# Opening of a transformer block on one core: four modulation blocks ahead of the first product instead of two

## The chip, the cores and the metric

One Trainium2 chip, one of its cores. The time is that of one execution on the device in microseconds, median of three runs. Engines are named as in the profile: PE is TensorE, ACT is ScalarE, DVE is VectorE, POOL is GpSimd, SP is SyncE, which issues most loads.

## The reference

The kernel computes one block of a transformer for 512 tokens of width 1024, in float32: a layer norm, a gated feed-forward (width 2816), a token mixer (pooling and three kinds of attention), and a second feed-forward, each followed by a layer norm and each entered by a modulation that depends on a vector c:

```python
x = layer_norm(x, ln_in_g, ln_in_b)
c_act = jax.nn.silu(c)
ada = (c_act @ w_ada[l] + b_ada[l]).reshape(c.shape[0], 3, 3, D_MODEL)
mod = lambda i, j: ada[:, i, j][:, None, :]
h = x * (1.0 + mod(0, 1)) + mod(0, 0)
x = layer_norm(ALPHA * x + 0.5 * mod(0, 2) * swiglu(h, ffn1_w_in[l], ffn1_w_out[l]), ln1_g[l], ln1_b[l])
```

The change is in what comes ahead of the first feed-forward and in its first products: the norm of x, mod(0, 0) and mod(0, 1) (shift and scale of h), and h itself.

## The kernel before

Everything is held transposed: X is eight tiles (m = 0 to 7) of 128 features x 512 tokens. A float32 product is made of three: a weight panel (128 x 1024, raw) is split into w_hi (ScalarE, L917) and w_lo (GpSimd, L433), h into h_hi (ScalarE, L967) and h_lo (VectorE, L1420), and TensorE multiplies h_hi by w_hi, h_lo by w_hi and h_hi by w_lo (L509 to L511, "a product" below: three matmuls). Raw panels have two slots, so panel p is loaded when panel p - 2 is split (L334).

**The order of the opening.** SyncE loads X in four pieces, then by the list FIRST_LOADS the panels ("p", i) of 512 KB and the modulation blocks ("a", k) of 1 MB (ada_first); block k holds the columns of w_ada that give shift and scale of tile k of h. TensorE sums X and its squares (first_norm, L559 and L561), turns the sums into columns (first_norm_columns, L570), VectorE makes mean and reciprocal deviation of them (with a square root on ScalarE), and TensorE spreads the two over all partitions (first_norm_row, L578, to banks 2 and 3).

For each block k: TensorE multiplies the block by c (first_modulation_rows, L540: 8 matmuls, 16 instructions), ScalarE copies the partial rows to arow (first_row, L942), TensorE sums them into columns (first_modulation_cols, L549), and VectorE makes mod of the columns (first_columns, L1410 to L1414; its last step counts up first_mod). Then ScalarE makes hbuf and h_hi of tile k (L962, L967), VectorE h_lo (L1420, which counts up h_split).

**The first products.** In feed_forward(1) six output tiles (banks 0 to 5) are summed at once, k outermost: for each k six products (18 matmuls), each waiting for h_split of its k. The eight panels' worth of weights is arranged so that the 48 products use panels 0 to 5 one after the other, eight products each. Rows of block k + AHEAD stand ahead of the products of k, its columns ahead of the product m = 3. AHEAD is 2, and the blocks use banks 6 and 7 in turn. ScalarE follows FIRST_SPLITS: behind first_row(k + AHEAD) it splits the panels listed for k and then makes h of tile k + 1. On all engines instructions are executed in the order of the program; each wait in it holds up what stands behind it on the same engine.

Behind the 48 products the feed-forward goes on with two banks at a time, and the rest of the kernel follows (mixer, second feed-forward).

Of the kernel before, what the change touches and what calls it, by code (L numbers as in the profile page):

```python
# [35 lines left out]
P = 128  # L36
D = 1024
T = 512
KT = D // P
# [55 lines left out]
FIRST_LOADS = [("p", 0), ("a", 0), ("a", 1), ("p", 1), ("a", 2), ("a", 3), ("p", 2), ("a", 4), ("a", 5), ("p", 3),  # L95
               ("a", 6), ("a", 7), ("p", 4), ("p", 5), ("p", 6)]

FIRST_SPLITS = [[1], [2], [3], [4], [], [5], [6], []]
AHEAD = 2
# [24 lines left out]
def build(nc, xT, cols, ada_w, ada1, ffn_in, ffn_out, mix_w, pool_w, branch_w, mixout_w,  # L124
          w1, w2, pos, ident_in, dist_in, cbias_in, cmask_in, icnt_in, out):
    with ExitStack() as ctx:
# [85 lines left out]
        ident_landed = sem("ident_landed")  # L212
# [118 lines left out]
        def _(sp):  # L331
# [54 lines left out]
            sp.dma_start(posv[:, :, :], pos[:, :, :]).then_inc(const_landed, 16)  # L386
            sp.dma_start(w2s[:, :, :, :], w2[:, :, :, :]).then_inc(const_landed, 16)
            sp.dma_start(icnt[:, :, :], icnt_in[:, :, :]).then_inc(const_landed, 16)
# [116 lines left out]
        def _(pe):  # L505
# [24 lines left out]
            def first_modulation_rows(k):  # L530

                b = 6 + k % 2
# [3 lines left out]
                if k >= 2:  # L536
                    pe.wait_ge(first_mod, k - 1)
# [6 lines left out]
            def first_modulation_cols(k):  # L544

                b = 6 + k % 2
# [48 lines left out]
            def feed_forward(n):  # L595
# [11 lines left out]
                for i in range(FIRST * KT):  # L607
# [5 lines left out]
                    if i == 1 and n == 1:  # L613
                        first_modulation_cols(1)
                    if m == 3 and n == 1 and k + AHEAD < KT:
                        first_modulation_cols(k + AHEAD)
                    if n == 1 and i == 2:
                        pe.wait_ge(rows_copied, 2)
                    if i % 8 == 0:
                        pe.wait_ge(split_done, base + i // 8 + 1)  # L620
# [41 lines left out]
            first_norm()  # L662
            first_norm_columns()
            first_modulation_rows(0)
            pe.wait_ge(ident_landed, 16)
# [3 lines left out]
            first_modulation_rows(1)  # L669
# [37 lines left out]
            pe.wait_ge(const_landed, 16 * 3)  # L707
# [196 lines left out]
        def _(act):  # L904
# [34 lines left out]
            def first_row(k):  # L939

                act.wait_ge(first_rows, k + 1)
                act.activation(arow[:, k, :], psum[:, 6 + k % 2, 0:2 * P],  # L942
                               ACT.Copy).then_inc(first_rows_taken, 1)

            def norm(L):

                act.wait_ge(var_done, L + 1)
                act.activation(st[:, 4, :], st[:, 3, :], ACT.Sqrt).then_inc(std_done, 1)
                if L == 0:
                    first_row(0)  # L950
# [6 lines left out]
                if L < 3:  # L957
# [11 lines left out]
                    if L == 0:  # L969
# [7 lines left out]
                        first_row(1)  # L977
                        todo[0] = 1
# [68 lines left out]
            act.dma_start(ident[:, :], ident_in[:, :]).then_inc(ident_landed, 16)  # L1047
# [133 lines left out]
        def _(dve):  # L1181
# [224 lines left out]
            def first_columns(k):  # L1406

                dve.wait_ge(first_cols, k + 1)
                shift_, scale_ = psum[:, 6 + k % 2, 2 * P:2 * P + 1], psum[:, 6 + k % 2, 2 * P + 2:2 * P + 3]
# [33 lines left out]
            first_low(0)  # L1443
            first_tile(1)
            first_columns(1)
            for m in range(1, KT):
# [3 lines left out]
                if m + 1 < KT:  # L1450
                    first_columns(m + 1)
# [318 lines left out]
```

## Time and profile before

| | us |
|---|---|
| median of 3 runs | 1177.31 (1176.4 to 1177.74) |
| the profiled execution | 1177.74 |
| its span, first to last instruction | 1175.6 |
| PE busy | 1117.5 (95%) |
| DVE busy | 522.4 (44%) |
| ACT busy | 399.7 (34%) |
| POOL busy | 540.8 (46%) |

The span is what the trace covers. A "PE busy" share of 95% is time in which some matmul was under way; matmuls overlap, so the start-to-start distance says more than the length of one. Times in a timeline count from the start of the span. A row of a timeline gives start and length in us, engine, line of the kernel, operation, what it writes and reads, how many; in brackets the idle time of the engine ahead of it and what ended that. Rows of loads give the time to issue in ns, first and last start in us, and the time from issue to landing. PEclk is the granted clock of TensorE as a share of 2.4 GHz.

### The profile page before, as it was taken

The numbers are of one execution on the slowest core, as the hardware profiler recorded it, in microseconds if no ns is written. First come the engines' busy times: TensorE is split into PE (matmuls) and PEld (weight loads), VectorE is DVE, ScalarE is ACT, GpSimd is POOL, SyncE is SP. The second block draws the span as 40 slices with busy tenths as digits, with TensorE's granted clock in tenths as the row PEclk, the third lists the DMA queues.
The fourth block names the chain that finished last, engine by engine and source line by source line (L and its number), as shares of the span: only waits on it lengthen the run. The fifth ranks groups of instructions, "written<-read, shape, count | busy, mean of one in ns | idle before, by whom it ended". The sixth has DMA issues, their size and how long they took to land.

```text
span 1175.6 us, 14482 instructions
## 1 busy us (share of the span) xinstructions
PE 1117.5 (95%) x5184; PEld 885.3 (75%) x5184; DVE 522.4 (44%) x829; ACT 399.7 (34%) x608; POOL 540.8 (46%) x268
## 2 busy tenths in 40 slices
PE   7999999999999699999999999969999999999992
PEld 4788888888888477865478888848888888888881
DVE  5577776111311564268837776661622221111116
ACT  4453322323222352247722233344323232222212
POOL 2434555444444352357815553544544544444423
PEclk9999999999999799999999999979999999999996
DMA  9455554323233621110036554313333332333311
GB/s 372 158 189 196 188 187 154 105 85 96 86 99 101 225 85 47 57 55 18 19 117 215 189 183 138 125 36 126 125 125 125 107 114 100 88 96 99 99 32 72
DMA packets 46991, 142.06 MB, mean 121 GB/s; under 512 B 5472, under 2 KB 5984, under 8 KB 45664
## 3 DMA queue, kind: packets, MB, share of 16 engines
q1 hardware_dynamic: 45936, 136.25, 35.0%
q10 hardware_dynamic: 1008, 5.17, 1.1%
q8 instruction: 30, 0.49, 0.2%
q14 instruction: 17, 0.14, 0.0%
HBM read 139.31 MB, written 2.10 MB: 120 GB/s over the span
## 4 chain that ended last, share of the span: by engine, by line
PE 77%; issue 10%; POOL 5%; DVE 5%; ACT 2%; DMA 0%; POOLq 0%; ACTq 0%; DVEq 0%
PE psum L509 24%; PE psum L511 24%; PE psum L510 24%; POOL w_lo L433 3%; PE psum L694 1%; POOL Pr L468 1%; POOL h_lo L491 1%; PE psum L593 1%; ACT Pr L1113 1%; PE psum L813 1%; DVE X L1284 1%; PE psum L526 0%; DMA X<-in_xT 0%; PE psum L540 0%; PE psum L762 0%
## 5 line engine op out<-in xcount | busy, mean ns | idle before, releaser
L433 POOL TENSOR_TENSOR w_lo<-raw,w_hi 128x1024 fp32r<-128x1024 f32 x184 | 453.7, 2471 | 547.6 <-ACT w_hi L917 547.3
L509 PE MATMUL psum<-h_hi,w_hi 128*128 128x512 f32 x952 | 375.3, 394 | 9.0 <-POOL h_lo L491 8.8
L511 PE MATMUL psum<-h_hi,w_lo 128*128 128x512 f32 x952 | 372.3, 391 | 0.0
L510 PE MATMUL psum<-h_lo,w_hi 128*128 128x512 f32 x952 | 372.2, 391 | 0.0
L917 ACT ACTIVATE w_hi<-raw 128x1024 fp32r<-128x1024 f32 x184 | 192.6, 1051 | 162.2 <-PE psum L511 103.2
L509 PEld LDWEIGHTS psum<-h_hi,w_hi 128*128 128x128 f32 x952 | 179.8, 189 | 54.9 <-POOL h_lo L491 9.5
L511 PEld LDWEIGHTS psum<-h_hi,w_lo 128*128 128x128 f32 x952 | 179.8, 189 | 38.1
L510 PEld LDWEIGHTS psum<-h_lo,w_hi 128*128 128x128 f32 x952 | 179.9, 189 | 36.5
L1312 DVE SCALAR_TENSOR_TENSOR acc<-ada_raw,cact,acc 128x512 f32<-128x512 f32 x98 | 145.3, 1517 | 19.3 <-DMA ada_raw<-in_ada_w 19.2
L509 PE MATMUL psum<-act_hi,w_hi 128*128 128x512 f32 x352 | 137.3, 390 | 0.0
L511 PE MATMUL psum<-act_hi,w_lo 128*128 128x512 f32 x352 | 137.0, 389 | 0.0
L510 PE MATMUL psum<-act_lo,w_hi 128*128 128x512 f32 x352 | 136.9, 389 | 0.0
L1380 DVE SCALAR_TENSOR_TENSOR X<-psum,mod,X 128x512 f32<-128x512 f32 x24 | 18.0, 750 | 217.4 <-PE psum L511 217.4
L1015 ACT ACTIVATE act_hi<-scr 128x512 f32 (+1 forms) x42 | 26.5, 632 | 194.2 <-DVE scr L1342 194.2
L1333 DVE SCALAR_TENSOR_TENSOR scr<-scr,psum 128x512 f32<-128x512 f32 x44 | 30.2, 686 | 108.6 <-ACT scr L1022 108.6
L511 PEld LDWEIGHTS psum<-act_hi,w_lo 128*128 128x128 f32 x352 | 66.1, 188 | 13.8
L510 PEld LDWEIGHTS psum<-act_lo,w_hi 128*128 128x128 f32 x352 | 66.1, 188 | 13.6
L509 PEld LDWEIGHTS psum<-act_hi,w_hi 128*128 128x128 f32 x352 | 66.1, 188 | 13.5
L1342 DVE TENSOR_TENSOR scr<-scr,psum 128x512 f32<-128x512 f32 x44 | 30.2, 686 | 89.0 <-PE psum L511 88.7
L1022 ACT ACTIVATE scr<-psum 128x512 f32<-128x512 f32 x44 | 26.0, 592 | 85.1 <-PE psum L511 85.1
L468 POOL TENSOR_SCALAR Pr<-Pr,pscl 128x128 f32<-128x128 f32 (+2 forms) x48 | 44.9, 954 | 19.2 <-DVE pscl L1585 19.2
L1324 DVE TENSOR_TENSOR act_lo<-scr,act_hi 128x512 f32 (+1 forms) x44 | 35.6, 808 | 36.7 <-ACT act_hi L1015 35.3
(205 smaller groups left out, 960.1 us busy)
## 6 DMA issues: line engine op xcount, KB each, us to landing
raw<-in_ffn_in SPq DMA_DIRECT2D x88, 512.0 KB, 3.3
ada_raw<-in_ada_w SPq DMA_DIRECT2D x112, 256.0 KB, 3.6
raw<-in_mix_w SPq DMA_DIRECT2D x31, 512.0 KB, 3.3
raw<-in_ffn_out SPq DMA_DIRECT2D x32, 448.0 KB, 3.3
ada_first<-in_ada SPq DMA_DIRECT2D x8, 1024.0 KB, 11.6
raw<-in_ffn_out SPq DMA_DIRECT2D x16, 512.0 KB, 3.5
raw<-in_branch_w SPq DMA_DIRECT2D x8, 512.0 KB, 4.0
raw<-in_mixout_w SPq DMA_DIRECT2D x8, 512.0 KB, 3.3
```

What stands on the lines that cost most here:

```text
L433: gp.tensor_tensor(w_lo[:, slot, :], raw[:, slot % 2, :], w_hi[:, slot, :].bitcast(F32), ALU.subtract).then_inc(split_done, 1)
L468: gp.tensor_scalar(pr, pr, pscl[:, n:n + 1], None, ALU.mult).then_inc(probs_pool, 1)
L509: pe.matmul(o_, w_hi[:, wslot, ws], xh, start=first, stop=False)
L510: pe.matmul(o_, w_hi[:, wslot, ws], xl, start=False, stop=False)
L511: return pe.matmul(o_, w_lo[:, wslot, ws], xh, start=False, stop=last)
L917: act.activation(w_hi[:, slot, :], raw[:, slot % 2, :], ACT.Copy).then_inc(split_hi, 1)
L1015: act.activation(act_hi[:, c - 1, :] if isinstance(c, int) else act_hi[:, bass.ds(c - 1, 1), :].rearrange("p o t -> p (o t)"), scr[:, 1 - ...
L1022: act.activation(scr[:, c2, :], bank(2 * c2 if b is None else b), ACT.Tanh, scale=0.5).then_inc(tanh_done, 1)
L1312: dve.scalar_tensor_tensor(a, ada_raw[:, q % 3, :], sc, a, ALU.mult, ALU.add).then_inc(ada_used, 1)
L1324: dve.tensor_tensor(lo_, scr[:, b, :], hi.bitcast(F32), ALU.subtract).then_inc(act_split, 1)
L1333: dve.scalar_tensor_tensor(scr[:, c2, :], scr[:, c2, :], 1.0, bank(b0), ALU.add, ALU.mult).then_inc(gated, 1)
L1342: dve.tensor_tensor(scr[:, c2, :], scr[:, c2, :], bank(b0 + 1), ALU.mult).then_inc(hidden_made, 1)
```

## The change

FIRST_LOADS loads blocks 2 and 3 ahead of panel 1, and blocks 4 and 5 ahead of panel 2. AHEAD becomes 4, and blocks 2 and 3 use banks 4 and 5 (FIRST_BANK), which products m = 4 and 5 need as well, hence two new waits for first_mod at k = 0. Ahead of the first product TensorE now does the rows of blocks 0 to 4 and the columns of blocks 0 to 3; the rows of block 0 stand ahead of the norm's columns. ScalarE splits panel 1 before it copies the rows of blocks 2 and 3, and FIRST_SPLITS becomes one k earlier for panels 2 to 6. The small constants posv (16 KB), w2s (128 KB) and icnt (32 KB) are loaded at the start from ScalarE's queue instead of by SyncE behind the first panels, with one semaphore for them and ident.

```diff
-FIRST_LOADS = [("p", 0), ("a", 0), ("a", 1), ("p", 1), ("a", 2), ("a", 3), ("p", 2), ("a", 4), ("a", 5), ("p", 3),
-               ("a", 6), ("a", 7), ("p", 4), ("p", 5), ("p", 6)]
-FIRST_SPLITS = [[1], [2], [3], [4], [], [5], [6], []]
-AHEAD = 2
+FIRST_LOADS = [("p", 0), ("a", 0), ("a", 1), ("a", 2), ("a", 3), ("p", 1), ("a", 4), ("a", 5), ("p", 2), ("a", 6),
+               ("a", 7), ("p", 3), ("p", 4), ("p", 5), ("p", 6)]
+FIRST_SPLITS = [[2], [3], [4], [5], [], [6], [], []]
+AHEAD = 4
+FIRST_BANK = [6, 7, 4, 5, 6, 7, 6, 7]
...
-            sp.dma_start(posv[:, :, :], pos[:, :, :]).then_inc(const_landed, 16)
-            sp.dma_start(w2s[:, :, :, :], w2[:, :, :, :]).then_inc(const_landed, 16)
-            sp.dma_start(icnt[:, :, :], icnt_in[:, :, :]).then_inc(const_landed, 16)
...
             def first_modulation_rows(k):
 
-                b = 6 + k % 2
+                b = FIRST_BANK[k]
                 pe.wait_ge(ada0_landed[k], 16)
                 if k == 0:
                     pe.wait_ge(cpad_made, 1)
-                if k >= 2:
-                    pe.wait_ge(first_mod, k - 1)
+                if k >= AHEAD:
+                    pe.wait_ge(first_mod, k - AHEAD + 1 if k < 6 else k - 1)
...
-                    if i == 1 and n == 1:
-                        first_modulation_cols(1)
                     if m == 3 and n == 1 and k + AHEAD < KT:
                         first_modulation_cols(k + AHEAD)
                     if n == 1 and i == 2:
                         pe.wait_ge(rows_copied, 2)
+                    if n == 1 and i in (4, 5):
+                        pe.wait_ge(first_mod, i - 1)
...
             first_norm()
+            first_modulation_rows(0)
             first_norm_columns()
-            first_modulation_rows(0)
-            pe.wait_ge(ident_landed, 16)
+            first_modulation_rows(1)
+            pe.wait_ge(const_landed, 16 * 4)
             first_norm_row(0)
             first_norm_row(1)
             first_modulation_cols(0)
-            first_modulation_rows(1)
+            first_modulation_cols(1)
+            for k in range(2, AHEAD):
+                first_modulation_rows(k)
+                first_modulation_cols(k)
             feed_forward(1)
...
             def norm(L):
 
+                if L == 0:
+                    first_row(0)
                 act.wait_ge(var_done, L + 1)
                 act.activation(st[:, 4, :], st[:, 3, :], ACT.Sqrt).then_inc(std_done, 1)
                 if L == 0:
-                    first_row(0)
+                    first_row(1)
...
-                        first_row(1)
-                        todo[0] = 1
+                        split(1, 1, 1)
+                        todo[0] = 2
+                        for k in range(2, AHEAD):
+                            first_row(k)
...
-            act.dma_start(ident[:, :], ident_in[:, :]).then_inc(ident_landed, 16)
+            act.dma_start(ident[:, :], ident_in[:, :]).then_inc(const_landed, 16)
+            act.dma_start(posv[:, :, :], pos[:, :, :]).then_inc(const_landed, 16)
+            act.dma_start(w2s[:, :, :, :], w2[:, :, :, :]).then_inc(const_landed, 16)
+            act.dma_start(icnt[:, :, :], icnt_in[:, :, :]).then_inc(const_landed, 16)
...
             first_low(0)
+            first_columns(1)
+            first_columns(2)
             first_tile(1)
-            first_columns(1)
+            first_columns(3)
             for m in range(1, KT):
                 if m + 1 < KT:
                     first_tile(m + 1)
                 first_low(m)
-                if m + 1 < KT:
-                    first_columns(m + 1)
+                if m - 1 + AHEAD < KT:
+                    first_columns(m - 1 + AHEAD)
```

TensorE, from the end of the sums to the first product, before (ada_first_61 is block 0, _62 block 1, and so on; ada0_landed0 is the landing of block 0, first_rows_taken a row copy of ScalarE):

```order
L570 MATMUL psum<-pick,sqsum 128x2 [waits x_sums_taken,pick_made]
L570 MATMUL psum<-pick,sqsum 128x2 x3
L540 MATMUL psum<-ada_first_61,cpad 32x256 [waits cpad_made,ada0_landed0]
...
L578 MATMUL psum<-ident,st 128x128 [waits stats_small,ident_landed]
...
L549 MATMUL psum<-ones,arow 128x2 [waits first_rows_taken]
...
L540 MATMUL psum<-ada_first_62,cpad 32x256 [waits ada0_landed1]
...
L540 MATMUL psum<-ada_first_63,cpad 32x256 [waits first_mod,ada0_landed2]
...
L509 MATMUL psum<-h_hi,w_hi 128x512 [waits split_done,h_split]
```

And after the change:

```order
L538 MATMUL psum<-ada_first_61,cpad 32x256 [waits cpad_made,ada0_landed0]
L538 MATMUL psum<-ada_first_61,cpad 32x256 x7
L568 MATMUL psum<-pick,sqsum 128x2 [waits x_sums_taken,pick_made]
...
L538 MATMUL psum<-ada_first_62,cpad 32x256 [waits ada0_landed1]
...
L538 MATMUL psum<-ada_first_63,cpad 32x256 [waits ada0_landed2]
L538 MATMUL psum<-ada_first_63,cpad 32x256 x7
L547 MATMUL psum<-ones,arow 128x2 [waits first_rows_taken]
...
L538 MATMUL psum<-ada_first_64,cpad 32x256 [waits ada0_landed3]
...
L547 MATMUL psum<-ones,arow 128x2 [waits first_rows_taken]
...
L538 MATMUL psum<-ada_first_65,cpad 32x256 [waits first_mod,ada0_landed4]
L538 MATMUL psum<-ada_first_65,cpad 32x256 x7
L507 MATMUL psum<-h_hi,w_hi 128x512 [waits split_done,h_split]
```

Two more blocks' rows and three more blocks' columns stand ahead of the first product, two of the columns behind row copies that ScalarE makes late, and block 0's rows have moved ahead of the norm's columns.

ScalarE, from the split of panel 0 to the making of h of tile 1, before (raw_landed1 is the landing of an odd panel):

```order
L917 ACTIVATE w_hi<-raw 128x1024 [waits raw_landed0]
L948 ACTIVATE st<-st 128x4 [waits var_done]
L942 ACTIVATE arow<-psum 128x256 [waits first_rows]
L971 ACTIVATE scr<-psum 128x512 [waits scaled]
L974 ACTIVATE h_hi<-X,mod 128x512 [waits first_mod,xhat_done]
L976 ACTIVATE scr<-psum 128x512
L942 ACTIVATE arow<-psum 128x256 [waits first_rows] x2
L917 ACTIVATE w_hi<-raw 128x1024 [waits raw_landed1]
L962 ACTIVATE hbuf<-X,mod 128x512 [waits first_mod,xhat_done]
```

And after the change:

```order
L918 ACTIVATE w_hi<-raw 128x1024 [waits raw_landed0]
L943 ACTIVATE arow<-psum 128x256 [waits first_rows]
L951 ACTIVATE st<-st 128x4 [waits var_done]
L943 ACTIVATE arow<-psum 128x256 [waits first_rows]
L974 ACTIVATE scr<-psum 128x512 [waits scaled]
L977 ACTIVATE h_hi<-X,mod 128x512 [waits first_mod,xhat_done]
L979 ACTIVATE scr<-psum 128x512
L918 ACTIVATE w_hi<-raw 128x1024 [waits raw_landed1]
L943 ACTIVATE arow<-psum 128x256 [waits first_rows] x3
L918 ACTIVATE w_hi<-raw 128x1024 [waits raw_landed0]
L965 ACTIVATE hbuf<-X,mod 128x512 [waits first_mod,xhat_done]
```

The split of panel 1 stands ahead of the row copies of blocks 2, 3 and 4, and the split of panel 2 ahead of the h of tile 1.

## Rows read from the trace of the kernel before

**Rows 1.** Busy time by stretch: start:end length, busy us (instructions) per engine, PEclk.
```profile
21.00:392.00 371.00, 370.92 (x1714) 304.20 (x1715) 163.25 (x192) 118.83 (x151) 172.11 (x70) 1.00 0.43 142
```

**Rows 2.** Timeline of TensorE up to the first product: start, length in us.
```profile
13.23 1.02 PE L570 MATMUL psum<-pick,sqsum 128*128 128x2 f32 x8 [0.88 <-DVE sqsum L1404]
...
14.18 1.07 PE L540 MATMUL psum<-ada_first,cpad 128*32 128x256 f32 x16
...
16.93 1.16 PE L578 MATMUL psum<-ident,st 128*128 128x128 f32 x8 [0.59 <-DVE st L1263]
...
19.81 1.07 PE L540 MATMUL psum<-ada_first,cpad 128*32 128x256 f32 x16 [0.38 <-DMA ada_first<-in_ada]
...
21.08 0.50 PE L509 MATMUL psum<-h_hi,w_hi 128*128 128x512 f32 x1 [0.20 <-DVE h_lo L1420]
```

**Rows 3.** Loads of blocks 0-3, panel 1, panel 2, blocks 4-5: issue, time to landing.
```profile
L385 SPq DMA_DIRECT2D ada_first<-in_ada x4: 432/491/685, 3.6 to 5.9; - x4
...
DMA to landing us min/median/max: 9.9/13.1/16.4
...
L335 SPq DMA_DIRECT2D raw<-in_ffn_in x1: 449/449/449, 4.9 to 4.9; - x1
...
DMA to landing us min/median/max: 12.4/12.4/12.4
...
L335 SPq DMA_DIRECT2D raw<-in_ffn_in x1: 327/327/327, 15.2 to 15.2; - x1
...
DMA to landing us min/median/max: 8.3/8.3/8.3
...
L385 SPq DMA_DIRECT2D ada_first<-in_ada x2: 432/432/433, 15.6 to 16.1; - x2
...
DMA to landing us min/median/max: 11.4/12.4/13.4
```

**Rows 4.** Timeline of TensorE: a block's rows, first products of k.
```profile
26.33 1.07 PE L540 MATMUL psum<-ada_first,cpad 128*32 128x256 f32 x16
...
27.33 0.50 PE L509 MATMUL psum<-h_hi,w_hi 128*128 128x512 f32 x1
...
50.56 0.50 PE L509 MATMUL psum<-h_hi,w_hi 128*128 128x512 f32 x1
...
55.27 0.39 PE L509 MATMUL psum<-h_hi,w_hi 128*128 128x512 f32 x1
...
59.39 0.39 PE L509 MATMUL psum<-h_hi,w_hi 128*128 128x512 f32 x1
```

**Rows 5.** Timeline of ScalarE: second broadcast copy, a row copy, a split.
```profile
20.14 0.58 ACT L976 ACTIVATE scr<-psum 128x512 f32<-128x512 f32 x1
...
27.47 0.38 ACT L942 ACTIVATE arow<-psum 128x256 f32<-128x256 f32 x1 [2.87 <-PE psum L540]
27.75 1.05 ACT L917 ACTIVATE w_hi<-raw 128x1024 fp32r<-128x1024 f32 x1
```

**Rows 6.** Timeline of GpSimd and VectorE: w_lo and h_lo beside it.
```profile
28.88 2.40 POOL L433 TENSOR_TENSOR w_lo<-raw,w_hi 128x1024 fp32r<-128x1024 f32 x1 [4.14 <-ACT w_hi L917]
...
30.20 1.63 DVE L1420 TENSOR_TENSOR h_lo<-hbuf,h_hi 128x512 fp32r<-128x512 f32 x1 [1.75 <-ACT h_hi L967]
```

**Rows 7.** Timeline of TensorE around the second norm, then stretches with their PEclk.
```profile
399.47 3.78 PE L593 MATMUL psum<-scr,ones 128*128 128x512 f32 x4 [3.81 <-DVE scr L1272]
...
407.05 0.77 PE L509 MATMUL psum<-h_hi,w_hi 128*128 128x512 f32 x1 [3.79 <-POOL h_lo L491]
...
410.18 0.63 PE L511 MATMUL psum<-h_hi,w_lo 128*128 128x512 f32 x1
...
410.61 0.63 PE L509 MATMUL psum<-h_hi,w_hi 128*128 128x512 f32 x1
...
409.00:412.00 3.00, 2.84 (x7) 2.05 (x8) 2.75 (x5) 3.00 (x5) 3.00 (x4) 0.50 0.00 0
412.00:414.00 2.00, 1.86 (x7) 0.99 (x5) 0.00 (x0) 2.00 (x5) 2.00 (x2) 0.87 0.00 0
```

More of the change, by code:

```diff
@@ L211, in build @@
         x_landed = [sem(f"x_landed{i}") for i in range(4)]
-        ident_landed = sem("ident_landed")
         const_landed = sem("const_landed")
@@ L544, in first_modulation_cols @@
             def first_modulation_cols(k):
-                b = 6 + k % 2
+                b = FIRST_BANK[k]
                 pe.wait_ge(first_rows_taken, k + 1)
@@ L705, in _ @@
             k8_panel("q0")
-            pe.wait_ge(const_landed, 16 * 3)
             pe.wait_ge(cmp_hidden_T, 1)
@@ L941, in first_row @@
                 act.wait_ge(first_rows, k + 1)
-                act.activation(arow[:, k, :], psum[:, 6 + k % 2, 0:2 * P],
+                act.activation(arow[:, k, :], psum[:, FIRST_BANK[k], 0:2 * P],
                                ACT.Copy).then_inc(first_rows_taken, 1)
             def norm(L):
+                if L == 0:
+                    first_row(0)
                 act.wait_ge(var_done, L + 1)
@@ L1408, in first_columns @@
                 dve.wait_ge(first_cols, k + 1)
-                shift_, scale_ = psum[:, 6 + k % 2, 2 * P:2 * P + 1], psum[:, 6 + k % 2, 2 * P + 2:2 * P + 3]
+                shift_, scale_ = psum[:, FIRST_BANK[k], 2 * P:2 * P + 1], psum[:, FIRST_BANK[k], 2 * P + 2:2 * P + 3]
                 link(dve.scalar_tensor_tensor(mod[:, 5, k:k + 1], scale_, first_b[:, k:k + 1], b0[:, k:k + 1],
@@ L1466, in _ @@
             dve.memset(Pc[:, :, :, N_CMP:CPAD], 0.0)
-            dve.wait_ge(const_landed, 16 * 3)
             for kv, name in enumerate(("kc", "vc")):
```

## The prediction, made before the changed kernel ran

> **What bounds the kernel now.** I read first the busy time by stretches: from 21 to 392 us TensorE is busy 370.92 of 371.00 us [rows 1]. The first feed-forward is one unbroken run of products, so whatever moves its first product, or puts work or a wait between products, moves the end by as much, as long as the stages behind it are the same; the diff touches nothing behind 64 us except waits that were long met. So the forecast is a timetable of the first 64 us.
>
> Then TensorE's timeline up to the first product [rows 2]. Its reader sees one chain: the column sums of the norm at 13.23 (after a gap of 0.88, so what went before ended at 12.35), the second broadcast row at 16.93, which waits for VectorE's small statistics, and the first product at 21.08, with a wait of 0.20 for h_lo. Between the links stand the row products of blocks 0 (14.18), 1 and 2 (19.81), about 1.0 us each, in time in which TensorE would wait anyway. From the norm's columns to the first product it is 7.85 us.
>
> Then the transfers [rows 3]. The four ada_first issued at 3.6 to 5.9 land 9.9 to 16.4 after issue: block 0 at 13.5, block 3 at 22.3. Panel 1, issued between blocks 1 and 2, lands at 4.9 + 12.4 = 17.3. Panel 2 lands at 15.2 + 8.3 = 23.5, block 4 at 15.6 + 11.4 = 27.0 and block 5 at 16.1 + 13.4 = 29.5. So the queue is full the whole time, transfers land in the order of their issue, and one block costs 2.5 us and one panel 1.25. (Block 4 took 3.5 behind panel 2: there was 1.0 us of lag that I can't name.) None of this delays products, since blocks 3 to 7 are asked for late.
>
> Last the loop over k. Its first products stand at 27.33, 50.56, 55.27 and 59.39 [rows 4]: 5.81 us for each k that holds a block's rows and columns (four of them), 4.71 for the last one with its columns (the rows stand ahead of its first product), 4.12 with neither.
>
> **The change, part by part.** I time everything against the profiled run of 1177.74 (span 1175.6), which is 0.4 above the median of 1177.31.
>
> *Rows of block 0 ahead of the norm's columns.* TensorE executes in order and now stands at block 0's landing, 13.5, before it may do the columns. Rows start at 13.6 instead of 14.18, take 1.0 (as 26.33 to 27.33 [rows 4]), and the columns start at 14.6 instead of 13.23: +1.35 for the statistics and all that hangs on them. h_lo for the first product is then ready at 22.4. Bounds: +0.1, if the block were there when the sums end (12.35 [rows 2]), and +1.8, if it lands later by the next item. Block 1's rows follow (landing 16.0 at one block behind block 0), end at 17.1, and the first broadcast at 18.1, just before the second may start (14.6 + 3.70 = 18.3): hidden.
>
> *The three small constants moved to ScalarE's queue at the start.* 16 + 128 + 32 KB now run among the first transfers. At 2.5 us a MB that is 0.43 us for everything that lands behind them; before they ran at 43 us beside an idle queue. Between 0 (they fill gaps of the ramp) and 0.9 (twice the time of their bytes). I take 0.43 for transfers. The wait for all four constants is asked for at 17, hidden.
>
> *Panel 1 behind blocks 2 and 3.* The bytes ahead of and in panel 1 are now those of block 3 before: 22.3 + 0.43 = 22.7 instead of 17.3. Before, ScalarE took this panel when it was long there. Now ScalarE is done with the second row copy (20.14 plus 0.58, later by 1.35: 22.1 [rows 5]) and waits 0.6.
>
> *The wait that this adds.* ScalarE's order is now split of panel 1, then row copies 2 and 3, and TensorE does columns 2 ahead of rows 3 and columns 3 ahead of rows 4, all of it ahead of the first product. So products wait for columns 2, those for row copy 2, that for the split, that for panel 1. Timetable: split 22.7 to 23.75; copy 2 (0.38, [rows 5]) to 24.1; columns 2, and rows 3 at 24.55; in the trace the copy starts 1.14 after its rows (26.33 [rows 4] to 27.47 [rows 5]) and ends 0.38 on, so copy 3 ends at 26.1; columns 3, and rows 4 at 26.55; first product 1.0 later (26.33 to 27.33, [rows 4]) at 27.55. Block 4 itself lands at 25.2, with the lag of 1.0 at 26.2, so it is no bound, by little. Queued behind the waiting TensorE is everything. The start moves by 27.5 − 21.08 = **+6.4**. Bounds: without the 0.43 it is 27.1 (+6.0); with 0.9 for the constants 28.0 (+6.9).
>
> The Trainium skill ("DMA: Bandwidth & Descriptors", section on queues, rings and completion order) says that completion is not first-in first-out for an issuing engine. The landings above are in order, so this trace does not show it. If panel 1 nevertheless landed as early as 17.3, ScalarE would be bound by itself at 22.1 and the sum below would be 0.6 smaller.
>
> *What leaves the loop.* Before, from first product to the end of k = 7: 59.39 + 4.12 − 21.08 = 42.4. Now k = 0, 1, 2 hold columns and rows of a block (5.81 each), k = 3 the last columns (4.71), k = 4 to 7 nothing (4.12): 38.6. That is **−3.8**. It needs that nothing else is late.
>
> *What is late next.* h of block 1 is made behind the split of panel 2 on ScalarE. Panel 2, blocks 4 and 5 are the same set of bytes as before, so panel 2 now lands when block 5 did: 29.5 + 0.43 = 29.95, instead of 23.5. From a split's start to the end of h_lo it was 27.75 to 31.83, 4.08 us (the h_lo of VectorE ends 0.55 after GpSimd's w_lo, [rows 5, 6]): h_lo 1 at 34.0. TensorE comes to it at 27.55 + 5.81 = 33.35: stall 0.7. Panel 3 now stands behind blocks 6 and 7: 29.95 + 2.5 + 2.5 + 1.25 = 36.2, h_lo 2 at 40.3, TensorE there at 34.0 + 5.8 = 39.8: stall 0.5. For k = 3 the row copy releases the split at 40.2, h_lo 3 at 44.3 against 46.1: hidden; the ones behind have no split or a spare 0.2. Together **+1.2**; bounds 0 (no lag, no shift: h_lo 1 at 32.6) and 2.5 (each 0.6 later).
>
> The new banks 4 and 5 make the products m = 4 and 5 wait for VectorE to have taken blocks 2 and 3. That is done by 27; nothing, unless VectorE is held by GpSimd's split of panel 1 (23.85 to 26.2), at most 0.5. The removed loads at 43 and removed waits are worth nothing, since they never ended a wait.
>
> Sum: +6.4 − 3.8 + 1.2 = **+3.8**, so 1181.5 against the profiled run and 1181.1 for a median.
>
> **Rivals.** *The clock falls.* By the timetable TensorE idles from about 21.3 to 24.15 after light work, 2.8 us. In the trace, behind an idle gap of 3.81 in the norm, the granted clock is 0.50 (1.2 GHz) and products start 0.43 apart (410.18 to 410.61 [rows 7]) instead of 0.23 (4.12 for 18 products, [rows 4]). Products began again at 407.05; the mean of 0.87 from 412 to 414 says that full speed (2.4 GHz) came back near 412.5, 5.4 us on. The gap of 0.88 in [rows 2] cost nothing: the 1.0 us per block behind it is that of the loop. The new gap lies between the two. Price: 0 to 12 products at 0.20 more, and slower rows, +3.3 at most; but slower products also swallow the 1.2 of stalls, since those are ends of other engines' work. I take +1.5: 1182.6. The Trainium skill ("TensorE: Matmul & The Clock Gate", Part 1) says the throttled state is the default and activity releases it; the trace agrees, and it makes this rival more than a remote one.
>
> *The timetable is right but everything lands early.* No shift by the constants, no lag: first product at 27.1, no stalls: +6.0 − 3.8 = +2.2, 1179.5, which is not slower than can be told. It decides at one point: panel 2 landed by 28.9 and panel 1 by 22.3. For it: the lag has no cause that I know. Against: the constants have to run somewhere in a full queue, and the lag was in the one trace there is. Even here the start can't come below 26.9, since ScalarE's split stands between the copies whenever its panel lands; so I see no way to a gain.
>
> *X lands later.* If the constants go ahead of X, the norm's sums end later too and the 0.43 counts twice: +4.7, 1182.0. The last sums stood about 1 us behind the landing of X, which covers it.
>
> **How the numbers follow.** Forecast 0.45 (own range 1180.3 to 1182.2), clock 0.32, early landings 0.15, X 0.05, and 0.03 for something that gives a gain. 0.2% is 2.35 us, about what a measurement of this kernel tells from no change, so the border is 1179.7. Slower: 0.45 + 0.32 + 0.05, less a little of the forecast's lower edge, and a third of the early case gives 0.80; within 0.17; faster 0.03. The range goes from 1178.8 (the early case with a fast median) to 1184.2 (the clock at its dearer end).
>
> **What would show it.** In the new profile: the norm's columns at 14.6 to 15.0 behind block 0's rows; panel 1 landed near 22.5; ScalarE idle before the split of panel 1; TensorE idle 2.5 to 3 us ahead of columns 2; first product at 27 to 28; gaps ahead of k = 1 and k = 2 of under 1 us with h_lo as releaser; 4.12 per k from k = 4; granted clock 1.00 in 20 to 30. Wrong if the first product stands before 25, if panel 1 lands out of order, or if something behind 64 us changes by more than the shift.

## The result, and the profile after

| | before | after |
|---|---|---|
| median | 1177.53 (1176.4 to 1178.65, 4 runs) | 1185.21 (1184.42 to 1186.39, 4 runs) |
| ratio, 95% interval | | 1.0064 (1.005 to 1.008) |
| the profiled execution | 1177.74 | 1185.08 |
| its span | 1175.6 | 1183.2 |

The change costs 7.7 us. The direction was forecast, the size was not: twice the 3.8 of the sum, and outside the range. The first product comes at 31.39 instead of 21.08, and the 48 products end at 71.67 instead of 63.47: 8.2 later. At the transposes of the next norm it is still 8.2 (402.69 against 394.49). By the spans 7.6 is left at the end. That last difference lies in stages that the change does not touch: from the end of the 48 to the end of the span it is 1111.2 to 1112.2 in nine profiles of kernels that have these stages alike (1112.15 before, 1111.53 after) and 1113.3 to 1113.9 in four (e2, e5, v1, v2), in which the granted clock was at 0.50 once more, for some us from about 492 on. So differences of 1 to 2 us between whole kernels say little by themselves; the timetable of the first 72 us says more.

TensorE after the change, from the end of the sums on (columns as in [rows 2]; L538 are a block's rows, L568 the norm's columns, L576 both broadcasts, L547 a block's columns, L507 the first of a product's three matmuls):

```profile
13.97 1.07 PE L538 MATMUL psum<-ada_first,cpad 128*32 128x256 f32 x16 [1.42 <-DMA ada_first<-in_ada]
14.97 1.05 PE L568 MATMUL psum<-pick,sqsum 128*128 128x2 f32 x8
...
17.46 2.05 PE L576 MATMUL psum<-ident,st 128*128 128x128 f32 x16
...
25.20 1.01 PE L547 MATMUL psum<-ones,arow 128*128 128x2 f32 x4 [3.90 <-ACT arow L943]
26.14 1.94 PE L538 MATMUL psum<-ada_first,cpad 128*32 128x256 f32 x16
...
29.52 1.94 PE L538 MATMUL psum<-ada_first,cpad 128*32 128x256 f32 x16
31.39 0.80 PE L507 MATMUL psum<-h_hi,w_hi 128*128 128x512 f32 x1
...
34.12 0.47 PE L507 MATMUL psum<-h_hi,w_hi 128*128 128x512 f32 x1
...
38.47 0.50 PE L507 MATMUL psum<-h_hi,w_hi 128*128 128x512 f32 x1
```

Against [rows 2] and [rows 4]: the rows of block 0 wait 1.42 for their block and the norm's columns start at 14.97, as forecast. Then TensorE idles 3.90 ahead of the columns of block 2. Behind the gap every piece takes longer, the small ones nearly twice as long: columns 1.01 instead of the 0.61 that they have in e1, a block's rows 1.94 instead of 1.07, the matmul of a product 0.80 instead of 0.50. From 34.12 on they are normal again. k = 0 takes 7.08 (31.39 to 38.47) instead of 5.81.

The loads of panel 1 and panel 2 (columns as in [rows 3]):

```profile
L336 SPq DMA_DIRECT2D raw<-in_ffn_in x1: 442/442/442, 5.8 to 5.8; - x1
...
DMA to landing us min/median/max: 18.0/18.0/18.0
...
L336 SPq DMA_DIRECT2D raw<-in_ffn_in x1: 328/328/328, 15.5 to 15.5; - x1
...
DMA to landing us min/median/max: 14.5/14.5/14.5
```

Panel 1 lands at 5.85 + 18.0 = 23.8 (forecast 22.7, before 17.3), panel 2 at 15.5 + 14.5 = 30.0 (forecast 29.95). The four blocks ahead of panel 1 landed 2.5 apart; panel 1 took 2.4 instead of 1.25, the same sort of lag of about 1.1 that block 4 had in [rows 3].

What goes with this lag stands in the view of the queues. From 19 to 24 us of the changed kernel, beside the loads of the program, there is one packet of the instruction queue (packets, MB, share of the 16 DMA engines' time):

```profile
q8 instruction: 1, 0.02, 1.4%
```

It is of 16 KB, begins at 21.64 and takes 1.08 us. Each of the 14 profiles has one such packet, begun between 20.5 and 23.2 us and 1.07 to 1.09 long, and no second one of that size ahead of 34 us; the transfer that is late, by 0.6 to 1.5, is each time the one under way or the next behind it. No experiment moves the packet, so that it causes the lag is likely and not shown.

ScalarE in the gap (answers [rows 5]): the second broadcast copy, the split of panel 1, the copies of block 2 and 3.

```profile
21.57 0.57 ACT L979 ACTIVATE scr<-psum 128x512 f32<-128x512 f32 x1
23.82 1.06 ACT L918 ACTIVATE w_hi<-raw 128x1024 fp32r<-128x1024 f32 x1 [1.68 <-DMA raw<-in_ffn_in]
24.79 0.36 ACT L943 ACTIVATE arow<-psum 128x256 f32<-128x256 f32 x1
28.14 0.38 ACT L943 ACTIVATE arow<-psum 128x256 f32<-128x256 f32 x1 [2.99 <-PE psum L538]
```

It is free at 22.1, waits 1.68 for panel 1, splits, and only then copies the rows that TensorE finished at 21.3. The new chain is the one of the forecast.

The granted clock by stretches (after the length come busy us and counts of PE, PEld, DVE, ACT and POOL, then PEclk, DMA share, GB/s):

```profile
20.00:24.00 4.00, 1.30 (x19) 0.63 (x18) 2.42 (x9) 1.47 (x3) 0.00 (x0) 1.00 1.02 416
24.00:28.00 4.00, 2.80 (x20) 1.53 (x20) 1.68 (x5) 1.15 (x2) 2.35 (x1) 0.50 1.00 412
28.00:32.00 4.00, 3.50 (x26) 2.05 (x23) 2.43 (x6) 0.86 (x3) 0.00 (x0) 0.50 1.01 418
...
34.00:38.00 4.00, 4.00 (x29) 2.96 (x32) 3.37 (x6) 0.22 (x1) 1.31 (x1) 0.97 0.47 165
72.00:392.00 320.00, 320.00 (x1426) 265.22 (x1425) 131.19 (x143) 92.11 (x114) 149.57 (x61) 1.00 0.41 130
```

From 24 to 34 it is 0.50, which is 1.2 GHz; the rows of the kernel before show that state only behind the norm's gap of 3.81 [rows 7]. It begins near 24.0, inside the gap, and ends near 34.2. From 72 to 392 TensorE is busy 320.00 of 320.00: the shift of the opening is carried whole.

### The profile page after: what moved, and what is told of

Same layout as the page of the kernel before. It is cut to its first block, busy times and chain, and to the rows that moved or that the text cites. A ratio compares the mean times of both kernels' runs of the same rounds, so it can differ in the third digit from the quotient of the medians.

```text
span 1183.2 us, 14478 instructions
## 1 busy us (share of the span) xinstructions
PE 1121.2 (95%) x5184; PEld 887.8 (75%) x5184; DVE 513.9 (43%) x829; ACT 400.5 (34%) x608; POOL 539.6 (46%) x268
## 4 chain that ended last, share of the span: by engine, by line
PE 87%; DVE 5%; ACT 2%; POOL 2%; issue 2%; DMA 2%; SPq 0%; ACTq 0%; DVEq 0%; POOLq 0%
PE psum L507 27%; PE psum L508 27%; PE psum L509 27%; DMA raw<-in_ffn_in 2%; PE psum L696 1%; POOL Pr L466 1%; POOL h_lo L489 1%; PE psum L591 1%; ACT Pr L1121 1%; PE psum L814 1%; PE psum L841 1%; PE psum L538 1%; DVE X L1292 1%; PE psum L524 1%; PE psum L763 0%
## 5 line engine op out<-in xcount | busy, mean ns | idle before, releaser
L507 PE MATMUL psum<-h_hi,w_hi 128*128 128x512 f32 x952 | 375.2, 394 | 9.2 <-POOL h_lo L489 9.0
L507 PEld LDWEIGHTS psum<-h_hi,w_hi 128*128 128x128 f32 x952 | 180.1, 189 | 55.7 <-POOL h_lo L489 9.9
L1320 DVE SCALAR_TENSOR_TENSOR acc<-ada_raw,cact,acc 128x512 f32<-128x512 f32 x98 | 137.0, 1435 | 16.6 <-DMA ada_raw<-in_ada_w 16.6
L507 PE MATMUL psum<-act_hi,w_hi 128*128 128x512 f32 x352 | 137.3, 390 | 0.0
L508 PEld LDWEIGHTS psum<-act_lo,w_hi 128*128 128x128 f32 x352 | 66.1, 188 | 13.6
L507 PEld LDWEIGHTS psum<-act_hi,w_hi 128*128 128x128 f32 x352 | 66.1, 188 | 13.5
## 6 DMA issues: line engine op xcount, KB each, us to landing
ada_first<-in_ada SPq DMA_DIRECT2D x8, 1024.0 KB, 16.3
```

Source lines behind the costliest of these rows:

```text
L507: pe.matmul(o_, w_hi[:, wslot, ws], xh, start=first, stop=False)
L508: pe.matmul(o_, w_hi[:, wslot, ws], xl, start=False, stop=False)
L1320: dve.scalar_tensor_tensor(a, ada_raw[:, q % 3, :], sc, a, ALU.mult, ALU.add).then_inc(ada_used, 1)
```

## The experiments

The notation: "end of the 48" is the start of the product behind k = 7, 63.47 before and 71.67 after. Ratios are to the kernel before on the same chip.

**e1: fill the gap.**

```diff
             for k in range(2, AHEAD):
                 first_modulation_rows(k)
+                if k == 2:
+                    for _ in range(4):
+                        pe.matmul(psum[:, 0, :], ones[:, :], hbuf[:, 7, :], start=True, stop=True)
                 first_modulation_cols(k)
```

> The changed kernel with four extra 128x512 matmuls on TensorE (their result goes to bank 0 and is overwritten) in the gap before the columns of block 2, so that TensorE does not idle there. Theory (wait plus clock): the gap of 3.90 brings the granted clock to 0.50 from 24 to 34 us; with the gap filled the clock stays at 1.00, rows 3 and 4 take 1.0 instead of 1.9, columns 0.45 instead of 0.94, the first product comes at 28.6 instead of 31.39 and k = 0 takes 5.8 instead of 7.1: about 4.0 less than the changed kernel, 1181.2. Rival (all of it is the landing of panel 1 and the order of engines, the clock costs nothing net since later waits take it back): within 0.5 of the changed kernel, 1185.2.

Measured: 1181.97, ratio 1.0043 (1.0027 to 1.006), against 1.0064 for the change. The extra matmuls are L673:

```profile
21.29 3.70 PE L673 MATMUL psum<-hbuf,ones 128*128 128x512 f32 x8
25.29 0.61 PE L547 MATMUL psum<-ones,arow 128*128 128x2 f32 x4 [0.30 <-ACT arow L946]
25.82 1.07 PE L538 MATMUL psum<-ada_first,cpad 128*32 128x256 f32 x16
...
28.93 0.50 PE L507 MATMUL psum<-h_hi,w_hi 128*128 128x512 f32 x1
```

```profile
24.00:32.00 8.00, 7.20 (x58) 4.65 (x57) 4.43 (x10) 3.99 (x7) 3.23 (x2) 1.00 1.02 419
```

Panel 1 landed at 23.9 here too, and columns 2 start at 25.29 as in the changed kernel (25.20). But the clock stays at 1.00, the rows of block 3 take 1.07, and from columns 2 to the first product it is 3.64 us instead of 6.19. End of the 48: 67.97, 3.7 less than after. The whole runs agree: 1181.70 to 1182.16 in e1 against 1184.32 to 1186.39 for the changed kernel, medians 3.2 apart; on e1's own chip e3, whose clock falls as in the changed kernel, has 1184.68 to 1186.49, medians 2.9 apart. By the two ratios it is 2.5, with intervals that overlap. The mean granted clock of a whole run is 0.980 in all four of e1 and 0.973 to 0.976 in all eight of the changed kernel on record, so the profiled runs are no exceptions. Nothing else was changed, so the fall of the clock costs about 3 of the 7.7, between 2.5 and 3.7. Without it the change costs what the forecast said, within the noise: 1.0043 of 1177 is 5.1 (3.2 to 7.1), by the end of the 48 it is 4.5.

**e2: the split of panel 1 behind the copies.**

```diff
-                        split(1, 1, 1)
-                        todo[0] = 2
                         for k in range(2, AHEAD):
                             first_row(k)
+                        split(1, 1, 1)
+                        todo[0] = 2
```

> The changed kernel with ScalarE's split of panel 1 behind the row copies of blocks 2 and 3 instead of ahead of them. Theory: the chain panel 1, split, copy 2, columns 2 is gone; columns 2 at 22.6, rows 3 to 24.0, rows 4 then wait for block 4, which lands at 26.3: first product 27.4 with the clock held, and h of tile 1 late by about 1.0: 1181.3; if the gaps of 1.2, 0.5 and 1.4 bring the clock down together, 1183.5. Rival (the rows of five blocks ahead of the first product are the cost, whatever ScalarE's order): first product not before 30, 1184 or more.

Measured: 1182.36, ratio 1.0043 (1.0026 to 1.0059).

```profile
22.78 0.61 PE L547 MATMUL psum<-ones,arow 128*128 128x2 f32 x4 [1.17 <-ACT arow L943]
...
26.11 1.07 PE L538 MATMUL psum<-ada_first,cpad 128*32 128x256 f32 x16 [0.61 <-DMA ada_first<-in_ada]
27.11 0.50 PE L507 MATMUL psum<-h_hi,w_hi 128*128 128x512 f32 x1
```

Columns 2 come at 22.78 and the first product at 27.11 (forecast 27.4), now with a wait of 0.61 for block 4, as the theory had it. Then h of tile 1 is late by 1.0, and the end of the 48 is 67.59. (The other three runs have a mean granted clock of 0.976 or 0.977, the profiled one 0.980, so whether the clock held in them is not known.) The wait on panel 1 thus cost the start 4.3 us, more than half of it through the clock (2.55, the 6.19 less the 3.64 of e1): with the wait but with the clock held (e1) the end is only 0.4 later than here. And with neither the wait nor the fall 4.1 are left by the end of the 48: the first product is 6.0 later than before, behind the landing of block 4 at 26.06, and the loop gives back 1.9.

**e3: the norm's columns ahead of the rows of block 0 again.**

```diff
             first_norm()
-            first_modulation_rows(0)
             first_norm_columns()
+            first_modulation_rows(0)
             first_modulation_rows(1)
```

> The changed kernel with the norm's columns ahead of the rows of block 0, as before. Theory: h of tile 0 is ready about 1.2 earlier, but the first product hangs on panel 1, so nothing changes: 1185.2 within 0.5. Rival (the forecast's first step as a term of its own): 1.3 less, 1183.9.

Measured: 1184.87, ratio 1.0067 (1.0051 to 1.0084): nothing gained.

```profile
13.78 1.02 PE L568 MATMUL psum<-pick,sqsum 128*128 128x2 f32 x8 [0.88 <-DVE sqsum L1412]
...
17.38 2.05 PE L576 MATMUL psum<-ident,st 128*128 128x128 f32 x16
...
31.39 0.80 PE L507 MATMUL psum<-h_hi,w_hi 128*128 128x512 f32 x1
```

The norm's columns are 1.2 earlier (13.78), but the broadcasts (L576) start at 17.38 as before the edit (17.46): they stand behind the rows of block 1, which wait for that block's landing. And the first product is the same anyway. So the first step of the forecast, +1.35, costs nothing: it is covered twice.

**e4: the old list of loads in the changed kernel** (FIRST_LOADS as in the lines with a minus in the diff above).

> The changed kernel with the old list of loads (panel 1 between blocks 1 and 2). Theory: panel 1 lands at 17.7, ScalarE splits it at 22.1 when it is free, columns 2 at 23.6, so the gap is 2.3 instead of 3.9; block 4 lands behind panel 2 at 27.6: first product 28.8. If a gap of 2.3 leaves the clock at 1.00: 1181.4. If it does not, slower rows and products: 1184. Rival (the loads are not the cause): 1185.2.

Measured: 1183.77, runs at 1181.95, 1182.36, 1185.19 and 1187.04, ratio 1.0068 (1.0046 to 1.009). TensorE, and the clock in one stretch:

```profile
23.23 0.61 PE L547 MATMUL psum<-ones,arow 128*128 128x2 f32 x4 [2.12 <-ACT arow L943]
...
29.29 0.80 PE L507 MATMUL psum<-h_hi,w_hi 128*128 128x512 f32 x1
```

```profile
24.00:28.00 4.00, 3.37 (x28) 1.72 (x28) 3.17 (x9) 0.38 (x1) 1.33 (x1) 0.50 1.00 416
```

Panel 1 lands at 17.5, and the gap is 2.12; yet the clock falls, near 23.8: the columns right behind the gap take 0.61, still fast, the first product 0.80 again, at 29.29. The end of the 48 is 68.87, 2.8 less than in the changed kernel. The theory left open what a gap of 2.3 does, and priced a fall at 1184. The profiled run has the fall and took 1181.95, the least of the four; so the fall in the opening is not what parts 1182 from 1185 to 1187, and the traces of the two dearer runs are not on record. By all four runs the order of loads by itself gives no gain that can be told (1.0068 against the 1.0064 of the change).

**e5: the new list of loads in the kernel before.**

> The kernel before with the new list of loads alone (two blocks ahead, the split of panel 1 where it was, behind the row copies 1 and 2). Theory: panel 1 lands at 22.3 to 23.4 (the small constants stay late), so ScalarE splits it late and h of tile 1 is ready at about 27.3 to 28.4 where TensorE asks for it at 27.3; panels 2 and 3 at 29.5 and 35.8 make h_lo 2 and 3 late by 0.5 to 1 each. The first product stays near 21.1, no idle gap long enough for the clock: 1 to 2.5 slower than before, 1178.2 to 1179.5. Rival (the new order of loads is the main cost of the change): 4 or more slower.

Measured: 1178.14 (10 runs), ratio 1.0003 (0.9993 to 1.0012). First product at 21.26 (a wait of 0.55 for h_lo, where it was 0.20), one more wait of 0.31 for h_lo ahead of k = 3, end of the 48 at 64.11, 0.6 later than before. Panels 2 and 3 landed at 29.3 and 35.5 as the theory had them; the cost is below its range. The loads alone are not the cost, since there ScalarE's copies and TensorE's first product don't stand behind panel 1.

**e6: the small constants late again.**

> The changed kernel with the three small constants loaded late by SyncE, as before. Theory: everything behind them lands 0.2 to 0.4 earlier, the gap before the columns of block 2 is shorter by as much, the clock still falls: 0.3 less than the changed kernel, 1184.9. Rival (they cause the late landing of panel 1, which came 1.1 later than the sum of bytes said): panel 1 at 22.3, 1.5 less, 1183.7.

Measured: 1184.45, ratio 1.0051 (1.0036 to 1.0067). Panel 1 landed at 22.5 without the lag, the gap was 2.74 and the clock fell all the same (0.50 from 24 to 34); end of the 48 at 71.00. The four runs span 2.8 us. The end of the 48 is 0.7 earlier than in the changed kernel, but this profile is also one without the lag on panel 1, so the 0.7 is not the price of the constants alone, and the intervals overlap. The constants don't make the lag of panel 1: e2 and e7 had the constants early and panel 1 at 23.0 and 22.7. The rival's 1.5 is not reached.

**e7: two extra matmuls instead of four.**

> The changed kernel with two extra matmuls in the gap before the columns of block 2 instead of four, so that about 2.2 us of it stay idle. Theory: a gap of 2.1 to 2.2 is near where the granted clock falls (it fell in the profile of the changed kernel with the old loads, with a gap of 2.12, whose runs lay at 1182 and at 1185 to 1187): runs on two levels, 1182 and 1185. Rival (only the landing of panel 1 counts): all runs at 1182 as with four.

Measured: 1181.17, ratio 1.0039 (1.0024 to 1.0054), all four runs between 1180.95 and 1182.70. In the profile the two matmuls (1.85 us) left 0.20 of the gap. The reason is a fall of the clock that had already happened:

```profile
14.04 1.07 PE L538 MATMUL psum<-ada_first,cpad 128*32 128x256 f32 x16 [1.95 <-DMA ada_first<-in_ada]
...
16.53 1.93 PE L538 MATMUL psum<-ada_first,cpad 128*32 128x256 f32 x16 [0.44 <-DMA ada_first<-in_ada]
...
21.82 1.07 PE L538 MATMUL psum<-ada_first,cpad 128*32 128x256 f32 x16
25.01 0.61 PE L547 MATMUL psum<-ones,arow 128*128 128x2 f32 x4 [0.20 <-ACT arow L946]
```

```profile
16.00:20.00 4.00, 3.56 (x25) 2.21 (x26) 1.50 (x9) 0.59 (x2) 0.00 (x0) 0.57 1.02 426
```

TensorE had idled 1.95 ahead of the rows of block 0 (1.42 in the changed kernel), the clock was at 0.50 from about 16.4 to 19.8, and the rows of block 2 came at 21.82 instead of 20.23. ScalarE was free only at 23.6, when panel 1 had long landed (22.7). So the run says that the clock stayed at 1.00 where hardly any idle time was left, and that 1.6 us lost in the middle of the opening cost nothing by the first product (28.66, against 28.93 in e1); it doesn't say where the clock falls. Inconclusive for its question.

**e8: rows of block 4 inside k = 0** (on top of e2).

```diff
-                        if n == 1 and k + AHEAD < KT:
+                        if n == 1 and k and k + AHEAD < KT:
                             first_modulation_rows(k + AHEAD)
                         pe.wait_ge(h_split, h0 + k + 1)
-                    if m == 3 and n == 1 and k + AHEAD < KT:
+                    if i == 2 and n == 1:
+                        first_modulation_rows(AHEAD)
+                    if m == (3 if k else 5) and n == 1 and k + AHEAD < KT:
```

> The changed kernel with ScalarE's split of panel 1 behind row copies 2 and 3, and the rows of block 4 moved from ahead of the first product to behind the second product of k = 0 (its columns ahead of the last product of k = 0). Theory (several landings in a row bound the opening): the first product comes at 25.3, but h of tile 1 hangs on the split of panel 2, landed at 29.8, so k = 1 starts at 34.0 as before the move and the time is that of the kernel with the split alone moved, 1182.3 within 0.7. Rival (the start is what counts): 1.5 to 2 less, 1180.5.

Measured: 1183.85, ratio 1.0059 (1.0043 to 1.0074).

```profile
26.52 0.78 PE L507 MATMUL psum<-h_hi,w_hi 128*128 128x512 f32 x1
...
35.16 0.50 PE L507 MATMUL psum<-h_hi,w_hi 128*128 128x512 f32 x1
```

```profile
27.00:29.00 2.00, 2.00 (x6) 1.32 (x5) 2.00 (x3) 0.00 (x0) 1.98 (x1) 0.50 1.07 436
```

The first product is at 26.52, 0.6 earlier than in e2 (1.8 was expected), but k = 1 starts at 35.16, 1.2 later. Here too the clock had fallen early, from about 16.3 to 19.7 behind a gap of 1.91, which made the columns of block 2 1.2 later than in e2 (23.94); it fell again at 26.5, so that k = 0 and the rows of block 4 in it ran partly at half clock. Panel 2 landed at 30.0, but ScalarE began its split at 31.04, behind the copy of those rows, and h_lo 1 was ready at 35.10, as TensorE came (35.04). So k = 1 hung on TensorE's own late rows of block 4 and not on the landing of panel 2, as the theory had it. The rival asked for a time near 1180.5, and no run reached it; but since two falls of the clock came with the edit, what the move is worth at full clock is not shown. The profiled run (1181.61) is the quickest of the four.

**e9: as e8, with the splits of panels 2 to 5 one k later** (FIRST_SPLITS = [[], [2], [3], [4], [5], [6], [], []]).

> As e8, and the splits of panels 2 to 5 one k later, so that h of tile 1 no longer waits for panel 2. Theory: k = 1 starts at 31.2 instead of 34.0, k = 4 at 50.5 or earlier, the end of the 48 products at 65 instead of 67.8: 2.5 less than e8, 1179.8, still 1.5 to 2.5 slower than before. Rival (panel 2 is not what binds k = 1): no change to e8.

Measured: 1182.81, 7 runs from 1178.34 to 1184.24, ratio 1.0045 (1.0031 to 1.0059). A miss: k = 1 starts at 34.90, and the end of the 48 is 67.65. h_lo 1 was ready at 33.1, so the splits no longer bind, but TensorE itself came only at 34.90, with the same two falls of the clock as in e8 (near 16.2 and 26.4). The one run at 1178.34 shows that the time of the theory can be reached; its trace is not on record.

**v1 and v2: extra matmuls ahead of X; in v2 block 2 ahead of panel 1 too** (in the kernel before).

```diff
             pe.wait_ge(memset_done, 1)
+            for _ in range(10):
+                pe.matmul(psum[:, 7, 0:P], ones[:, :], ones[:, :], start=True, stop=True)
             first_norm()
```

> The kernel before with ten extra 128x128 matmuls of ones on TensorE from 1 us on, before X has landed; their result goes to bank 7 and is overwritten. Theory: in the kernel before the sums of the norm run at half pace from 5.88 to 9.3 and end at 12.35, 1.9 behind the last squares; with TensorE at full pace earlier they end near 11.4, so the norm's chain is 0.9 shorter; but the rows of block 2 land at 19.8 and stand ahead of the first product: 0.2 less than before. Rival (pace of the sums is hidden by the landing of block 0 at 13.5): no change.

> As v1, and block 2 is loaded ahead of panel 1 (lands at 18.5). Theory: the first product comes at 20.2 instead of 21.08: 0.9 less than before, 1175.9 at a before of 1176.8. Rival: no change, since rows of block 0 or the copies of ScalarE end last.

Measured: 1178.94 (ratio 1.0006, 0.9997 to 1.0016) and 1178.8 (1.0006, 0.9997 to 1.0015): no gain. In v2 the norm's columns were 0.77 earlier than in [rows 2], the first product was not; VectorE and GpSimd tell why:

```profile
12.46 1.02 PE L570 MATMUL psum<-pick,sqsum 128*128 128x2 f32 x8 [0.88 <-DVE sqsum L1406]
...
21.10 0.50 PE L509 MATMUL psum<-h_hi,w_hi 128*128 128x512 f32 x1 [0.55 <-DVE h_lo L1422]
```

```profile
13.73 1.51 DVE L1245 TENSOR_TENSOR st<-st 128x4 f32<-128x4 f32 x1
```

```profile
12.87 2.36 POOL L433 TENSOR_TENSOR w_lo<-raw,w_hi 128x1024 fp32r<-128x1024 f32 x1 [11.69 <-ACT w_hi L919]
```

VectorE's first small operation on four numbers per partition (L1245) lasts 1.51 us and ends with GpSimd's w_lo of panel 0 (12.87 + 2.36 = 15.23). The other traces have the same end: 14.50 + 0.73 = 15.23 beside GpSimd's 15.21 in the kernel before, 14.98 beside 14.96 in v1. So the norm hangs on that split, not on the pace of the sums. (In v1 the clock also fell, from about 13.6 to 17.0, with no gap longer than 0.88 between the extra matmuls and the fall; in v2 it did not, and the first product came no earlier either.)

**v3: extra matmuls in the gaps of the later norms** (in the kernel before).

```diff
                     ins.then_inc(stats_ready, 1)
+                hold = 5 if L == 2 else 0
+                for _ in range(15):
+                    pe.matmul(bank(hold, P), ones[:, :], ones[:, :], start=True, stop=True)
                 for i in range(2):
                     pe.wait_ge(rows_made, 2 * L - 1 + i)
                     pe.matmul(bank(6 + i), ones[:, :], scr[:, i, :], start=True, stop=True).then_inc(rows_ready, 1)
+                if L < 3:
+                    for _ in range(15):
+                        pe.matmul(bank(hold, P), ones[:, :], ones[:, :], start=True, stop=True)
```

> The kernel before with fifteen extra 128x128 matmuls of ones on TensorE in each of the idle gaps of 3.8 us of the three later norms (behind the statistics, and behind the two broadcast rows in the first two of them); their result goes to a bank that is overwritten. Theory (the granted clock falls in these gaps): it stays at 1.00; the broadcasts take 2.0 instead of 3.8 in three norms, 1.7 each on the path, and the first products of the second feed-forward run at 0.23 instead of 0.43 for some 5 us, 2.5: 6 to 8 faster than before, 1169 to 1171. In the mixer the products wait for h_lo anyway and gain little. Rival (TensorE's pace in the norm is hidden by the other engines): no change.

Measured: 1171.13 (1170.67 to 1173.38), ratio 0.9952 (0.9939 to 0.9966): faster than both kernels, by 0.48% and by some 1.1%. TensorE around the second norm, and two stretches:

```profile
395.16 3.51 PE L593 MATMUL psum<-ones 128*128 128x128 f32 x30
399.13 1.98 PE L596 MATMUL psum<-scr,ones 128*128 128x512 f32 x4 [0.46 <-DVE scr L1278]
400.95 3.51 PE L599 MATMUL psum<-ones 128*128 128x128 f32 x30
405.25 0.47 PE L509 MATMUL psum<-h_hi,w_hi 128*128 128x512 f32 x1 [0.79 <-POOL h_lo L491]
```

```profile
394.00:404.00 10.00, 9.39 (x70) 8.14 (x71) 8.56 (x23) 1.90 (x4) 0.17 (x1) 1.00 1.00 388
774.00:784.00 10.00, 9.54 (x72) 8.19 (x70) 8.56 (x22) 2.24 (x4) 0.51 (x1) 1.00 0.03 12
```

The same stretches in the kernel before:

```profile
394.00:404.00 10.00, 4.95 (x12) 2.02 (x12) 7.19 (x20) 0.42 (x2) 0.00 (x0) 0.74 0.97 380
774.00:784.00 10.00, 4.66 (x12) 1.70 (x9) 7.18 (x20) 0.91 (x2) 0.00 (x0) 0.69 0.01 4
```

The two broadcasts (L596, four passes) take 1.98 instead of the 3.78 of [rows 7], the wait ahead of them shrinks to 0.46, and the clock is 1.00 where it was 0.74 and 0.69. It is not held for good: among the first products behind the second norm, with waits of 0.79, 1.17 and 0.24, it fell to 0.50 from about 408.2 to 411.6, and it fell once more near 490. The gain, 5.6 us by the ratio, is a little under the 6 to 8 that were expected.

## Why the prediction was wrong

- *Bound* (the first feed-forward is unbroken, so a shift is carried whole): right, 320.00 of 320.00.
- *Rows of block 0 ahead of the columns, +1.35*: the columns moved by 1.74 (14.97), near the upper bound; 1.2 of it is the order (e3), the rest a later landing of X. The step costs nothing (e3). It did not enter the sum, since the start was set by the other chain.
- *Constants, 0.43 later*: about right in size (block 0 lands 0.4 later). What it is worth in time was not separated from the lag (e6, 0.7 for both by the end of the 48).
- *Panel 1 and the wait it adds*: the mechanism is right (ScalarE waits, TensorE behind it). The landing was mis-sized: 23.8 instead of 22.7, +1.05. I had seen a lag of 1.0 in the trace and charged it to block 4 alone, where it was covered. In the new order panel 1 is due at 22.7, and in five of the nine profiles with it in that place (after, e1, e3, e8, e9) the lag was its own; in e2, e5, e6 and e7 it was block 4's.
- *From columns 2 to the first product*: this is the term that failed. Forecast 24.15 to 27.55, 3.4 us; measured 25.20 to 31.39, 6.19. e1, with the same landing and the same order, has 3.64. The sum priced these pieces at full clock, and they ran at half. The start is +10.3 instead of +6.4: 1.05 by panel 1, 2.55 by the clock, 0.24 because the pieces take a little more than the timetable even at full clock.
- *What leaves the loop, −3.8, and what is late next, +1.2*: 40.28 from first product to the end, against 42.39 before, so −2.1 instead of −2.6. Half clock in k = 0 cost 1.27; in return h_lo 1 and 2 were no longer late, as the text on the rival said; they are not late in e1 either (34.08, and TensorE comes at 34.74), so the lag of panel 1 alone covers the +1.2. e2, with an earlier start, shows the stalls of the forecast (1.0 and 0.3 with h_lo as releaser).
- *The rival "the clock falls"* was what happened. It had a chance of 0.32 and a price of 1.5, with 3.3 at most; by e1 the fall costs 2.55 in the start and 1.27 in k = 0. The price left out most of what four pieces between the gap and the first product lose at half clock, and the gap was longer (3.90 instead of 2.8) since panel 1 was late. With what was measured its sum is 3.8 + 2.8 + 1.3 − 1.2 + 1.05 = 7.75, against 8.2 by the end of the 48; the rest is in k = 4 and 5 (4.48 and 4.21 instead of 4.12). What the Trainium skill ("TensorE: Matmul & The Clock Gate", Part 1) says, that activity is what holds the full clock, agrees with these runs: 0.50 in e4 and after, 1.00 in e1.

So the sum without a falling clock, +3.8, is close to e1 (+4.5 by the end of the 48), partly by chance: e1's start is 1.45 later than forecast, and its loop 0.8 shorter. The cause of the miss is settled by e1: two disturbances, one that the trace showed and I covered, one that I priced too low.

What stays open is what brings the clock down. The length of the gap ahead of it does not decide it: in the opening the clock fell behind gaps of 3.90, 2.74 and 2.12 (after, e6, e4), and behind 1.95, 1.91 and 1.85 (e7, e8, e9, near 16 us), but also in v1 with none above 0.88; it stayed behind 1.42 and 1.33 (after and e1, in the same place), behind 1.52 and then 1.17, 0.50 and 0.61 (e2), while in e8 and e9 it fell a second time behind 1.17 and 0.50. That the instruction packet causes the lag in the landings is not shown either.

## What to carry to other kernels

A wait put ahead of dense work costs more than its length when it makes TensorE idle: look up what the clock does behind the existing gaps, and price every piece up to the return of the clock at the slow rate, the small ones first. Moving work of a saturated engine ahead of its first product can gain only what fits into idle time that is already there; here that was 2 us (the gaps of 0.88, 0.59, 0.38 and 0.20 in [rows 2]), and the blocks had not even landed. Where a profile shows half clock behind a gap that can't be closed, throw-away matmuls in it are worth a try (5.6 us here). All that were tried here were shorter than the gap; longer ones would stand in the way of the work behind it.

## What the runs showed of the hardware

- The granted clock fell behind gaps of 2.12 and 2.74 us as it did behind 3.9 (e4, e6, after), behind 1.85 to 1.95 at another place (e7, e8, e9), and in v1 with no gap above 0.88; a gap of 1.17 is followed by 1.00 in e2 and by 0.50 in e8. It can begin inside the gap (after, 24.0) or behind the first work after it (e4, 23.8).
- With matmuls of ones by ones, result unused, in the gaps of the norms the clock stayed at 1.00 for two stretches of ten microseconds with no other work than the norm's (v3), where it was 0.74 and 0.69 without them.
- VectorE's tensor_tensor on 128x4 took 1.51 us beside a GpSimd split, against 0.16 for its neighbours, and ended with it, within 0.02 us in the kernel before, v1 and v2.
- In every one of the profiles one transfer that lands between 23.1 and 27.1 us takes 0.6 to 1.5 us longer than its bytes, whichever it is: block 4 in [rows 3], panel 1 after the change (23.8), block 3 in e4 (23.8). A 16 KB packet of the instruction queue, 1.08 us long, begins 2.2 to 4.2 us ahead of that landing each time.
